# The dilated attention rebuilt for pairs of heads, and a fused bias-and-maximum pass in both attentions

## The chip, the cores and the metric

One NeuronCore of a Trainium2 chip runs the whole program. The metric is the device time of one execution in microseconds (us). The engines are TensorE (PE; PEld is its weight load), VectorE (DVE), ScalarE (ACT), GpSimd (POOL) and SyncE (SP), each with its own instruction stream; they meet only at semaphores.

## The reference

The program computes two transformer blocks over 512 tokens of width 1024 in fp32. The part that matters here is the second block, whose first layer holds a dilated attention beside a gated delta rule, and whose second layer holds a differential attention beside a gated linear attention:

```python
SWA_CONFIGS = ((128, 1), (512, 4), (2048, 16))
...
    s = jnp.einsum('bgnqhd,bgnkhd->bgnhqk', qb, kb).astype(jnp.float32) * dh ** -0.5
    s = s + bias.astype(jnp.float32)
    s = jnp.where(mask[None, None, :, None], s, -jnp.inf)
    m = jnp.max(s, axis=-1, keepdims=True)
    p = jnp.exp(s - m)
    l = jnp.sum(p, axis=-1, keepdims=True)
    o = jnp.einsum('bgnhqk,bgnkhd->bgnqhd', (p / l).astype(v.dtype), vb)
...
        s = jnp.einsum('bhcqd,bhckd->bhcqk', q_blk, kt).astype(jnp.float32) * dh ** -0.5
        s = jnp.where(dist >= 0, s + bias[None, :, None], -jnp.inf)
        p = jax.nn.softmax(s, axis=-1)
        attn = p[:, :, 0] - lam * p[:, :, 1]
```

Both attentions have 4 heads with keys of width 64. In the dilated one the three groups are merged by their log-sum-exp, which is the same as one softmax over the keys of all three. The kernel does it that way: for one head and one of the 4 residue classes of tokens (128 tokens each) there are 512 + 128 + 128 = 768 scores for each token.

## The kernel before

The program is a chain of regions, each closed by a barrier of all engines. Projections multiply in a split form (high and low parts, three matmuls, L292 to L294 and L315 to L317) with weights that SP loads ahead, ACT splits (L220) and DVE splits (L230). Around the change stand three of these regions.

`residual_region` ends with the projections for the dilated attention, "swa_qk" and "swa_v". ACT empties the banks of "swa_v" (L3193). Between the wait for the last group and its four copies ACT issues eight small DMAs (L3190), which load the bias tables of the two outer groups (`g12_bias`); four others for the inner group (`g0_bias`) are issued earlier (L3183). ACT waits at the end of the region for all twelve.

`attention` is a general softmax attention. For the dilated attention it gets 16 items, one per head and residue class. In an item PE makes three score matmuls into two PSUM banks (L620), with weights read in steps of 4 elements from `cls`; all three have the same 64 partitions for a head. DVE scales and adds the bias in three passes (L665), takes the maximum over 768 columns (L673), negates it (L676), and, when ACT has made the exponentials (L688), inverts the sums (L641) and scales all 768 columns (L651). PE turns six blocks of 128x128 (L597), ACT copies them out of PSUM in two passes (L698), PE multiplies by the values (L611, the values are the weights, the turned probabilities stream), and ACT copies the 64x128 result (L708). Scores have two pairs of banks, so PE works one item ahead: its order for step t is scores(t+1), turns(t-1), values(t-2).

`odd_mixer_region` runs the differential attention in 16 items, 4 heads times 4 query blocks with w = 128, 256, 384 and 512 keys, with the steps of the gated linear attention laid between them (on PE: inside, turn_inside, turn_keys, output, state, gla_sums). Each item has two softmaxes of width w. DVE: two bias passes (L2950, L2951), two maxima (L2954, L2956), a negation (L2958), then for the item before it the reciprocals (L2964) and two weighting passes (L2965, L2967), on which PE's turns wait (L2728). DVE's bias passes of item t wait in turn for the turns of item t-2.

The cross attention of the first block also uses `attention`, with other items.

## Time and profile before

| | before |
|---|---|
| runs | 2953.57, 2957.06, 2961.91 us (median 2957.06) |
| the profiled execution | 2957.7 us, its span 2955.4 us |
| mean granted TensorE clock | 0.958 |
| PE busy / PEld busy | 2722.0 us (92%) / 2178.0 us (74%) |
| DVE / ACT / POOL busy | 1594.1 (54%) / 1058.7 (36%) / 448.6 us (15%) |
| dilated attention, PE's first work to ACT's last copy | 1534.33 to 1614.70 us |
| attention of the odd layer, DVE's first work to its last weighting pass | 2401.28 to 2480.96 us |

PE is near full nearly everywhere, so a gain must be looked for stage by stage: in a stage in which PE is full only its own work counts, in one in which it waits the chain of waits does. A busy time of PE is modelled at its ends; starts are the surer numbers.

### The profile page before, as it was taken

What the parts mean: (1) busy time and instruction counts of PE and PEld (TensorE: products, weight loads), DVE (VectorE), ACT (ScalarE), POOL (GpSimd) and SP (SyncE); (2) the same over time, 40 slices, a digit from 0 to 9 for tenths busy, and PEclk for the clock granted to TensorE, in tenths of its full rate; (3) what the DMA queues carried; (4) which work ended last, traced back from release to release, by engine and by line L of the source; (5) the groups of instructions that cost most, each with busy time, mean ns of one, the idle gap of its engine ahead of it and who ended that gap; (6) DMA issues with size and microseconds to landing.
All of it is one profiled execution on the core that took longest, in us unless ns stands there. A gap on an engine that the chain in (4) does not pass through costs nothing. (4 is left out here: it accounts for less than half of the span.)

```text
span 2955.4 us, 33329 instructions
## 1 busy us (share of the span) xinstructions
PE 2722.0 (92%) x13110; PEld 2178.0 (74%) x13110; DVE 1594.1 (54%) x2249; ACT 1058.7 (36%) x1614; POOL 448.6 (15%) x359
## 2 busy tenths in 40 slices
PE   6998999789899999969989998899998987899997
PEld 4676999567678888746777896687786854687776
DVE  3735665444446652364435674666734256566743
ACT  4653332533342322334324343322224346422222
POOL 4544443001010000000000442000020031300002
PEclk9999899899999999989979999999999989999999
DMA  4424000433023323222220001122232210222231
GB/s 144 144 87 142 1 1 1 167 94 99 29 86 100 100 90 98 77 71 72 79 85 1 1 1 44 63 87 92 91 110 97 93 51 1 69 88 93 93 104 61
DMA packets 82626, 222.09 MB, mean 75 GB/s; under 512 B 13293, under 2 KB 29950, under 8 KB 81284
## 3 DMA queue, kind: packets, MB, share of 16 engines
q1 hardware_dynamic: 76960, 204.96, 22.0%
q10 hardware_dynamic: 5512, 15.01, 1.5%
q8 instruction: 105, 1.72, 0.2%
q14 instruction: 49, 0.39, 0.0%
HBM read 213.60 MB, written 11.58 MB: 76 GB/s over the span
## 5 line engine op out<-in xcount | busy, mean ns | idle before, releaser
L230 DVE TENSOR_TENSOR w_low<-w_raw,w_high 128x1024 fp32r<-128x1024 f32 (+2 forms) x338 | 407.2, 1206 | 884.2 <-ACT w_high L220 884.0
L292 PE MATMUL bank<-x_high,w_high 128*128 128x512 f32 x1840 | 744.9, 405 | 46.5 <-DVE x_low L486 20.4
L293 PE MATMUL bank<-x_low,w_high 128*128 128x512 f32 x1840 | 735.7, 400 | 0.0
L294 PE MATMUL bank<-x_high,w_low 128*128 128x512 f32 x1840 | 732.7, 398 | 0.0
L220 ACT ACTIVATE w_high<-w_raw 128x1024 fp32r<-128x1024 f32 (+2 forms) x380 | 386.2, 1019 | 631.6 <-PE bank L294 507.2
L292 PEld LDWEIGHTS bank<-x_high,w_high 128*128 128x128 f32 x1840 | 350.1, 190 | 159.3 <-issue 61.5
L293 PEld LDWEIGHTS bank<-x_low,w_high 128*128 128x128 f32 x1840 | 350.0, 190 | 88.1 <-issue 5.8
L294 PEld LDWEIGHTS bank<-x_high,w_low 128*128 128x128 f32 x1840 | 349.3, 190 | 83.6
L292 PE MATMUL bank<-f_high,w_high 128*128 128x512 f32 x528 | 208.8, 395 | 0.9 <-DVE w_low L230 0.9
L294 PE MATMUL bank<-f_high,w_low 128*128 128x512 f32 x528 | 209.1, 396 | 0.0
L293 PE MATMUL bank<-f_low,w_high 128*128 128x512 f32 x528 | 209.1, 396 | 0.0
L230 POOL TENSOR_TENSOR w_low<-w_raw,w_high 128x1024 fp32r<-128x1024 f32 x42 | 102.9, 2452 | 137.6 <-ACT w_high L220 137.6
L292 PEld LDWEIGHTS bank<-f_high,w_high 128*128 128x128 f32 x528 | 99.1, 188 | 27.9 <-issue 3.3
L293 PEld LDWEIGHTS bank<-f_low,w_high 128*128 128x128 f32 x528 | 99.1, 188 | 24.6 <-issue 0.5
L294 PEld LDWEIGHTS bank<-f_high,w_low 128*128 128x128 f32 x528 | 99.1, 188 | 23.2
L403 POOL TENSOR_TENSOR ln_half<-x 128x512 f32<-128x512 f32 x4 | 6.9, 1717 | 704.6 <-DVE x L3491 704.6
L3416 ACT ACTIVATE f_high<-gate 128x512 fp32r<-128x512 f32 x44 | 27.8, 632 | 215.0 <-DVE gate L3522 215.0
L292 PE MATMUL bank<-o_high,w_high 128*128 128x512 f32 x192 | 78.8, 410 | 17.6 <-DVE o_low L555 17.6
L3413 ACT ACTIVATE gate<-gate 128x512 f32<-128x512 f32 x44 | 27.8, 632 | 155.1 <-DVE gate L722 155.1
L1014 DVE TENSOR_TENSOR raw<-bank,rstd 128x512 f32<-128x512 f32 x38 | 25.9, 687 | 105.4 <-PE bank L294 80.0
L2001 POOL TENSOR_TENSOR bt<-m_ab,level_mask 128x512 f32<-128x512 f32 x48 | 65.9, 1380 | 84.5 <-PE bank L1612 83.1
L294 PE MATMUL bank<-o_high,w_low 128*128 128x512 f32 x192 | 77.4, 403 | 0.0
(593 smaller groups left out, 4319.9 us busy)
## 6 DMA issues: line engine op xcount, KB each, us to landing
w_raw<-in_ffn_in_dram SPq DMA_DIRECT2D x132, 512.0 KB, 3.4
w_raw<-in_ffn_out_dram SPq DMA_DIRECT2D x48, 512.0 KB, 3.6
w_raw<-in_gdn_in_dram SPq DMA_DIRECT2D x24, 512.0 KB, 3.4
w_raw<-in_mix_in_dram SPq DMA_DIRECT2D x22, 512.0 KB, 4.1
w_raw<-in_ffn_out_dram SPq DMA_DIRECT2D x24, 384.0 KB, 3.1
w_raw<-in_swa_qk_dram SPq DMA_DIRECT2D x12, 512.0 KB, 3.5
bias_rows<-bias_row ACTq DMA_DIRECT2D x4, 1280.0 KB, 14.0
w_raw<-in_mix_gate_a_dram SPq DMA_DIRECT2D x8, 512.0 KB, 3.4
```

What stands on the lines that cost most here:

```text
L220: self.nc.scalar.activation(self.high[c % SPLIT][:, 0:w], self.raw[c % RAW][:, 0:w], ACT.Copy).then_inc(self.high_done, 1)
L230: (on or self.nc.vector).tensor_tensor(self.low[c % SPLIT][:, 0:w], self.raw[c % RAW][:, 0:w], self.high[c % SPLIT][:, 0:w].bitcast(F32), ...
L292: nc.tensor.matmul(out, wh, high[:, k, :], start=first + at == 0, stop=False)
L293: nc.tensor.matmul(out, wh, low[:, k, :], start=False, stop=False)
L294: last = nc.tensor.matmul(out, wl, high[:, k, :], start=False, stop=first + at == depth - 1)
L403: self.nc.gpsimd.tensor_tensor(self.half[:], self.x[:, 0, :], self.x[:, 1, :], ALU.add).then_inc(self.S["half_ok"], 1)
L1014: W.freed(nc.vector.tensor_tensor(raw[i % 3][:], W.bank(PS, name, n)[:], rstd[:], ALU.mult), name, n)
L2001: nc.gpsimd.tensor_tensor(group(BT, g), group(MT[n % 2], g), mask[:, level:level + 1, :].broadcast_to([P, N, P]), ALU.mult).then_inc(R["ma ...
L3413: nc.scalar.activation(g[i % 2][:], g[i % 2][:], ACT.Silu).then_inc(R["act_ready"], 1)
L3416: nc.scalar.activation(FH[:, i, :], g[i % 2][:], ACT.Copy).then_inc(R["f_high"], 1)
```

## The change

`attention` keeps its work for the cross attention and loses the argument for loads. The dilated attention gets a region of its own, `window_region`, with 8 units, each one residue class of a pair of heads (head 0 of the pair on partitions 0 to 63, head 1 on 64 to 127):

- Scores: six matmuls, the two heads in turn, into banks 0 and 2 (the inner group) and 1 and 3 (the outer ones). There is no second set of banks: the scores of unit u+1 wait until DVE has read those of unit u.
- Logits: a fused DVE operation, `tensor_tensor_reduce`, adds the bias to the scores, multiplies by -1, and keeps the minimum, which serves as the negated maximum; ACT's exponential takes `scale=-1.0`. Two for each head: the inner 512 columns, and the outer 256, which start from the minimum of the first. The scale 1/8 moves to the queries where they are projected (`scaled_query` on DVE, and an ACT scale in the odd layer).
- Values: now the turned probabilities are the weights (128x128) and the values stream (64 columns), so the result has tokens on partitions, and DVE divides by the sums on the 128x128 result (`window_rows`) in place of scaling all columns. Four such results are turned by PE at the end of a head pair and ACT writes them out.
- Two of the three banks of turned blocks are copied by ACT, the third by DVE.
- The eight loads of `g12_bias` are issued by SP at the start of the new region, and DVE waits for the four of its head pair before the first outer pass.

The odd layer's attention takes the same fused operation for its two softmaxes (w columns each) in place of two bias passes, two maxima and a negation. The layer norms are alike in both kernels.

```diff
+def window_region(nc, C, PS, E, qk, vs, G0, G12, O, biases, masks, loaded):
...
+            for b in range(2):
+                for dst, src in biases[4 * b:4 * b + 4]:
+                    sp.dma_start(dst, src).then_inc(R[f"bias{b}"], 16)
...
+            def scores(u):
+                b, r = unit(u)
+                if u:
+                    pe.wait_ge(R["logits"], 2 * u)
+                for h in range(2):
+                    o = half(h)
+                    nc.tensor.matmul(PS[2 * h][:], cls[o, b, :, r], qk[o, 6 + b, :], start=True, stop=True)
+                for g in (1, 2):
+                    for h in range(2):
+                        o = half(h)
+                        last = nc.tensor.matmul(PS[2 * h + 1][:, chunk(g - 1)], cls[o, 2 * g + b, :, r],
+                                                cls[o, 6 + 2 * g + b, :, r], start=True, stop=True)
...
+                        last = nc.tensor.matmul(PS[7][:, o], PT[q // 4][:, chunk(q % 4)], v, start=j == 0, stop=j == PARTS - 1)
...
+            for u in range(N + 2):
+                if u < N:
+                    scores(u)
+                if u >= 2:
+                    values(u - 2)
+                if 1 <= u <= N:
+                    turn(u - 1)
+                if u >= 2 and (u - 2) % SWA_DIL == SWA_DIL - 1:
+                    finish((u - 2) // SWA_DIL)
...
+            for u in range(N + 2):
+                if 1 <= u <= N:
+                    copies(u - 1)
+                if u < N:
+                    exponentials(u)
...
+            for u in range(N + 2):
+                if u < N:
+                    logits(u)
+                if u >= 2:
+                    out(u - 2)
+                if 1 <= u <= N:
+                    last_copy(u - 1)
+                    inverse(u - 1)
...
-                steps(nc.vector.scalar_tensor_tensor(L[p][:, 0:w], PS[2 * p][:, 0:w], 64 ** -0.5, bias, ALU.mult, ALU.add))
-                nc.vector.scalar_tensor_tensor(L[p][:, w:2 * w], PS[2 * p + 1][:, 0:w], 64 ** -0.5, bias, ALU.mult,
-                                               ALU.add).then_inc(R["logits"], 1)
-                steps.wait()
-                steps(nc.vector.reduce_max(nmax[:, p, 0:1], L[p][:, 0:w], AX_X))
-                dve.wait_ge(R["logits"], t + 1)
-                steps(nc.vector.reduce_max(nmax[:, p, 1:2], L[p][:, w:2 * w], AX_X))
-                steps.wait()
-                nc.vector.tensor_scalar(nmax[:, p, :], nmax[:, p, :], -1.0, None, ALU.mult).then_inc(R["max"], 1)
+                for i in range(2):
+                    last = nc.vector.tensor_tensor_reduce(L[p][:, i * w:(i + 1) * w], PS[2 * p + i][:, 0:w], bias, -1.0, 3e38,
+                                                          ALU.add, ALU.min, nmax[:, p, i:i + 1])
+                last.then_inc(R["logits"], 1)
...
-                if gr:
-                    for dst, src in keep["biases"][1]:
-                        act.dma_start(dst, src).then_inc(R["biases"], 16)
```

PE in the middle of the dilated attention, one item and the scores that follow it, before (`logits` are the probabilities, `swa_v` the values; a matmul of this list is two records in the trace where both operands are fp32, a turn, with `ident`, is one):

```order
L620 MATMUL bank<-swa_qk_6786 128x512
L620 MATMUL bank<-swa_qk_6786 128x128 x2
L597 MATMUL bank<-ident,logits_222 128x128 x6
L611 MATMUL bank<-probs_turned_225,swa_v_6787 64x128 x6
L620 MATMUL bank<-swa_qk_6786 128x512
L620 MATMUL bank<-swa_qk_6786 128x128 x2
```

The same place after, one unit, which is the work of two items:

```order
L1465 MATMUL bank<-swa_qk_6783 128x512 x2
L1469 MATMUL bank<-swa_qk_6783 128x128 x4
L1498 MATMUL bank<-swa_v_6784,window_turned_12158 128x64 x4
L1498 MATMUL bank<-swa_v_6784,window_turned_12159 128x64 x4
L1498 MATMUL bank<-swa_v_6784,window_turned_12160 128x64 x4
L1480 MATMUL bank<-ident,window_logits_12156 128x128 x12
L1465 MATMUL bank<-swa_qk_6783 128x512 x2
L1469 MATMUL bank<-swa_qk_6783 128x128 x4
```

The score matmuls of two heads now stand beside one another, the result of a value matmul has 128 rows and 64 columns in place of 64 and 128, and the values come ahead of the turns.

ACT at the end of `residual_region` and the start of the attention, before:

```order
L220 ACTIVATE w_high_7<-w_raw_1 128x1024
L3190 DMA g_bias_6792<-bias_rows 128x128 x8
L3193 ACTIVATE swa_v_6787<-bank,rstd_cols_6795 128x4x128 x4
L543 UNCONDITIONAL_BRANCH
L681 UNCONDITIONAL_BRANCH
L688 ACT_TABLE_LOAD
L688 ACTIVATE logits_222,tot<-logits_222,nmax 128x768
```

And after:

```order
L220 ACTIVATE w_high_7<-w_raw_1 128x1024
L3346 ACTIVATE swa_v_6784<-bank,rstd_cols_6792 128x4x128 x4
L543 UNCONDITIONAL_BRANCH
L1517 UNCONDITIONAL_BRANCH
L1530 ACT_TABLE_LOAD
L1530 ACTIVATE window_logits_12156,tot_12164<-window_logits_12156,nmax_12163 128x768 x2
```

The eight DMAs have gone from between the last split of weights and the copies of `swa_v`; SP issues them behind the barrier.

DVE in the odd layer, one item with w = 384, before:

```order
L2950 SCALAR_TENSOR_TENSOR logits_19562<-bank,full_bias_6793 128x384
L2951 SCALAR_TENSOR_TENSOR logits_19562<-bank,full_bias_6793 128x384
L2954 TENSOR_REDUCE nmax_19573<-logits_19562 128x1
L2956 TENSOR_REDUCE nmax_19573<-logits_19562 128x1
L2958 TENSOR_SCALAR nmax_19573<-nmax_19573 128x2
L2984 SCALAR_TENSOR_TENSOR state_19568<-state_19568,gend_15065,bank 128x128 x2
L2964 RECIPROCAL tot_19574<-tot_19574 128x2
L2965 TENSOR_SCALAR logits_19563<-logits_19563,tot_19574,lam 128x256
L2967 SCALAR_TENSOR_TENSOR logits_19563<-logits_19563,tot_19574 128x256
```

And after, where the fused operation is printed as ISA, and each is followed by a second instruction that writes its minimum:

```order
L3112 ISA logits_19419,nmax_19430<-bank,full_bias_6790 128x384
L3112 ISA nmax_19430 128x1
L3112 ISA logits_19419,nmax_19430<-bank,full_bias_6790 128x384
L3112 ISA nmax_19430 128x1
L3140 SCALAR_TENSOR_TENSOR state_19425<-state_19425,gend_14922,bank 128x128 x2
L3120 RECIPROCAL tot_19431<-tot_19431 128x2
L3121 TENSOR_SCALAR logits_19420<-logits_19420,tot_19431,lam 128x256
L3123 SCALAR_TENSOR_TENSOR logits_19420<-logits_19420,tot_19431 128x256
```

Five instructions ahead of `state` have become four, two of them one column wide; what follows is unchanged.

## Rows read from the trace of the kernel before

**Rows 1.** Windows of both attentions: busy us (x instructions), PEclk, DMA share, GB/s.

```profile
core 0: us, PE busy (x) PEld busy (x) DVE busy (x) ACT busy (x) POOL busy (x), PEclk, DMA share, GB/s
1526.00:1534.30 8.30, 0.57 (x3) 0.26 (x2) 1.23 (x1) 3.48 (x5) 0.00 (x0) 0.70 0.49 129
1534.30:1552.00 17.70, 16.80 (x48) 11.25 (x48) 10.27 (x26) 6.11 (x11) 0.00 (x0) 0.50 0.09 28
1552.00:1562.00 10.00, 10.00 (x51) 7.73 (x51) 5.37 (x12) 4.74 (x11) 0.00 (x0) 0.94 0.00 0
2401.20:2481.00 79.80, 58.80 (x430) 37.40 (x430) 65.66 (x166) 47.77 (x142) 26.54 (x47) 0.90 0.02 5
```

**Rows 2.** Timeline, one item at full clock (start, us, engine, line; idle before).

```profile
1578.81 1.87 PEld L620 LDWEIGHTS bank<-swa_qk 64*128 64x128 f32 x6 [0.17 <-DVE logits L665]
1579.90 0.94 ACT L688 ACTIVATE logits<-logits,nmax 128x768 f32<-128x768 f32 x1 [0.59 <-DVE nmax L676]
1580.74 0.19 ACT L688 ACTIVATION_READ_ACCUMULATOR logits<-logits,nmax 128x1 f32 x1
1580.90 0.64 PEld L597 LDWEIGHTS bank<-ident,logits 128*128 128x128 f32 x6 [0.23 <-issue]
1581.71 1.28 PEld L611 LDWEIGHTS bank<-probs_turned,swa_v 128*64 128x64 f32 x12 [0.17 <-issue]
1581.88 1.09 DVE L665 SCALAR_TENSOR_TENSOR logits<-bank,g_bias 128x512 f32<-128x512 f32 x3 [1.29 <-PE bank L597]
1583.16 0.30 PEld L620 LDWEIGHTS bank<-swa_qk 64*128 64x128 f32 x1 [0.17 <-DVE logits L665]
```

**Rows 3.** Timeline, the end of the region ahead and its barrier, with the DMAs' landing.

```profile
1526.70 3.71 ACTq L3190 DMA_DIRECT2D g_bias<-bias_rows  x8
1527.76 1.23 DVE L230 TENSOR_TENSOR w_low<-w_raw,w_high 128x1024 fp32r<-128x1024 f32 x1 [4.42 <-ACT w_high L220]
1530.45 2.42 ACT L3193 ACTIVATE swa_v<-bank,rstd_cols 128x512 f32<-128x512 f32 x4 [2.73 <-issue]
1534.33 0.30 PEld L620 LDWEIGHTS bank<-swa_qk 64*128 64x128 f32 x1 [8.07 <-issue]
...
DMA to landing us min/median/max: 1.8/2.3/3.7
```

**Rows 4.** Timeline, values at half clock, and the last copy of the dilated attention.

```profile
1549.34 2.42 PEld L611 LDWEIGHTS bank<-probs_turned,swa_v 128*64 128x64 f32 x12 [0.33 <-issue]
...
1614.31 0.39 ACT L708 ACTIVATE o_even<-bank 64x128 f32<-64x128 f32 x1 [0.91 <-PE bank L611]
```

**Rows 5.** Timeline of PEld, two neighbouring loads of the outer scores.

```profile
1579.89 0.54 PEld L620 LDWEIGHTS bank<-swa_qk 64*128 64x128 f32 x2
```

**Rows 6.** Timeline of PE, score pairs of the odd layer (w = 128 and 512).

```profile
2440.02 0.30 PEld L2718 LDWEIGHTS bank<-diff_qk 64*128 64x128 f32 x4 [0.76 <-issue]
2440.02 0.49 PE L2718 MATMUL bank<-diff_qk 64*128 64x128 f32 x4
...
2454.82 1.13 PE L2718 MATMUL bank<-diff_qk 64*128 64x512 f32 x4
```

**Rows 7.** Timeline of PEld, loads of 128x128 under matmuls of 64 columns.

```profile
404.14 1.87 PEld L1534 LDWEIGHTS bank<-v_rows,m_ak 128*128 128x128 f32 x16
```

**Rows 8.** Timeline of DVE in the odd layer: items with w = 128, 384 and 512.

```profile
2462.62 0.29 DVE L2950 SCALAR_TENSOR_TENSOR logits<-bank,full_bias 128x128 f32<-128x128 f32 x1
2462.83 0.28 DVE L2951 SCALAR_TENSOR_TENSOR logits<-bank,full_bias 128x128 f32<-128x128 f32 x1
...
2463.61 0.16 DVE L2964 RECIPROCAL tot<-tot 128x2 f32<-128x2 f32 x1
...
2470.62 0.56 DVE L2950 SCALAR_TENSOR_TENSOR logits<-bank,full_bias 128x384 f32<-128x384 f32 x1 [2.21 <-PE bank L2728]
...
2474.95 0.69 DVE L2950 SCALAR_TENSOR_TENSOR logits<-bank,full_bias 128x512 f32<-128x512 f32 x1 [0.61 <-PE bank L2728]
2475.55 0.68 DVE L2951 SCALAR_TENSOR_TENSOR logits<-bank,full_bias 128x512 f32<-128x512 f32 x1
...
2477.45 0.17 DVE L2958 TENSOR_SCALAR nmax<-nmax 128x2 f32<-128x2 f32 x1
2477.53 0.16 DVE L2964 RECIPROCAL tot<-tot 128x2 f32<-128x2 f32 x1
```

**Rows 9.** Who waited for DVE's second weighting pass (L2967): us, times.

```profile
  PEld bank L2728: 23.9, 13
```

More of the change, by code:

```diff
@@ L566, in deep_blocks, with attention @@
         [(n, part)] for n in range(2, ND) for part in range(3)]
-def attention(nc, C, PS, items, width, values, loads=(), loaded=None):
+def attention(nc, C, PS, items, width, values):
     with stage(nc, "scores_ready", "logits_ready", "max_ready", "exp_ready", "probs_ready", "turned", "turned_sb",
@@ L582, in attention @@
         N = len(items)
-        @block.sync
-        def _(sp):
-            for dst, src in loads:
-                sp.dma_start(dst, src).then_inc(loaded, 16)
         @block.tensor
@@ L2703, in tile_of @@
         return t // NT, t % NT, (t % NT + 1) * P
-    with region(nc, "scores", "logits", "max", "exp", "probs", "turned", "turned_sb", "pv", "out", "own", "a_sums", "k_turned",
+    with region(nc, "scores", "logits", "exp", "probs", "turned", "turned_sb", "pv", "out", "own", "a_sums", "k_turned",
                 "o_sums", "s_sums", "d_sums", "g_sums", "rows_turned", "rows_ok", "am", "a_turned", "ker", "o", "o_sq", "d_sq", "g_read", "d_read", "log", "rstd", "at", "st",
@@ L3278, in _, with scaled_query @@
             dve.wait_ge(R["last_sq_ok"], ND)
+            def scaled_query(n):
+                W.split_low(dve, W.ahead("swa_qk", n))
+                W.wait(dve, "swa_qk", n)
+                W.freed(nc.vector.scalar_tensor_tensor(qk[:, n, :], W.bank(PS, "swa_qk", n)[:], SWA_DIM ** -0.5, rstd2[:],
+                                                       ALU.mult, ALU.mult), "swa_qk", n)
             for n in range(12):
-                scaled_to(qk[:, n, :], "swa_qk", n)
+                if n < 6:
+                    scaled_query(n)
+                else:
+                    scaled_to(qk[:, n, :], "swa_qk", n)
                 if 1 <= n < 4:
@@ L3669, in build @@
         loaded = nc.alloc_semaphore("masks_loaded")
[L3670 to L3688 removed]
+        pairs = near[1::3] + near[2::3]
+        window_region(nc, C, PS, E, qk, vs, G0, G12, OE, [pairs[i + 4 * j] for i in range(4) for j in range(2)],
+                      [(level_mask[:], A["level_mask"]), (pick[:], A["pick"])], loaded)
         recurrence_region(nc, C, PS, E, QKVZ, BETA, GAM, OE, {"level_mask": level_mask, "pick": pick, "loaded": loaded})
```

142 lines of the change are left out of this document (117 added, 25 removed).

## Prediction

> **What bounds the two stages now.** I read the windows first, then the timeline inside each stage, then who waits for whom. In the dilated attention PE is full: at half clock (PEclk 0.50) for the first 18 us, with PE 16.80 us busy of 17.70, and at full clock from about 1553 on, since the window 1552 to 1562 shows 0.94, which is 1.2 us at half [rows 1]. One item then takes 4.35 us (1578.81 to 1583.16), in which PE does scores for 2.09 us (to 1580.90), turns for 0.81 and values for 1.45 [rows 2]. PE's scores wait for DVE's bias passes by a margin that hardly shows (0.17 us), so PE's own work is the bound, and what counts is how much of it there is. The stage lasts from 1534.33 to 1614.70, 80.4 us [rows 3, 4]; 16 items of 4.35 us are 69.7, and the other 10.7 are half clock, fill and drain.
>
> In the odd layer it is otherwise. There DVE is busy 65.66 of 79.80 us, PE 58.80 and ACT 47.77 [rows 1], and PE's turns wait for DVE's second weighting pass in 13 of 16 items, 23.9 us in all [rows 9]. DVE waits back for the turns, 0.61 us in an item of 512 keys [rows 8]. The ring goes bias passes, maxima, weighting, turns, so DVE time taken out of it comes off the stage, except where another chain ends later: before the item with w = 384 DVE waits 2.21 us [rows 8], and there PE had the matmuls of the linear attention to do first.
>
> **Dilated attention, PE's work for one unit (two items).** *Scores.* Two neighbouring strided loads of the outer groups start 0.23 us apart (0.54 for two of 0.31) [rows 5], which is what an outer score record costs; the inner score streams 512 columns twice, 0.86 us for a matmul by the difference below. What two heads on different partitions do is shown in the odd layer: a pair of 128 columns takes 0.49 us and one of 512 takes 1.13, that is 0.64 for 384 columns more or 0.21 for 128, where four passes of 128 columns at 2.4 GHz are 0.21 for one matmul alone; and its four loads end after 0.30 us [rows 6]. So the pair runs side by side, loads too. I price scores at one load 0.22, the inner pair 0.86, four steps of 0.22 for the outer pairs and 0.2 of hand-over: 2.15 us, against 4.18 in two items. If the strided loads of the two halves took turns it would be eight steps, 3.0 us; with no overlap at all 4.2. I take the low value, since the pair of rows 6 has the same shape and only the step is new.
>
> *Turns.* Six load in 0.64, about 0.10 each; twelve and a hand-over are 1.4 us, against 1.62 [rows 2].
>
> *Values.* 24 records with weights of 128x128 and 64 moving columns. Sixteen such loads take 1.87 us, so 0.112 apart [rows 7]: 24 are 2.7, with the hand-over 2.85, against 2.90 now. Nothing is won there.
>
> A unit is then 6.4 us against 8.7.
>
 With the 0.11 of rows 7 for a step, a unit would be 0.55 us shorter and the stage 4.4 us; rows 5 show 0.23 for the strided one, and the sum goes by the row.
>
> *Does anything else become late?* With one set of score banks, the scores of unit u+1 wait for DVE's logits of unit u, while PE does values and turns, 4.25 us. DVE's logits are four fused passes. No trace here has the operation. Its bounds: as fast as the bias pass it replaces (0.60 from start to start at 512 columns, 0.21 at 128, so 0.34 at 256) [rows 8], or bias pass and maximum one after the other, double that. I take the first, as one pass over one PSUM and one SBUF operand. The second instruction, which writes the minimum, I put at 0.1, between the 0.08 from L2958 to L2964 [rows 8] and ACT's accumulator read of 0.19 [rows 2]. Logits: 2 x 0.60 + 2 x 0.34 + 4 x 0.1 = 2.3 us, hidden under 4.25. DVE's unit with its copy out of PSUM (as a pass of 512, 0.60), product and reciprocal is some 3.6, ACT's (two exponentials at 0.84 + 0.19 [rows 2], two copies of 512 columns taken at DVE's 0.60) some 3.3; both below 6.4. ACT begins exponentials of u only after the copies of u-1, but the turns that need them are 5 us off.
>
> *Fill, clock, drain.* Full clock came 18.9 us after PE began; I let it come after 17. At half clock values take 0.21 a load (2.42 for 12) [rows 4], 5.3 us a unit. The new order is scores 0 (3.1), a wait for the logits of 0 (2.6), scores 1, turns 0 (2.9), scores 2, and values 0 to 45% when the clock rises. That is 9.1 us of full-clock work in 17: 7.9 lost. At the end: copies out (0.9), the last product (0.35), four turns (0.6) and ACT's write (0.6), and 0.6 for the four turns in the middle: 3.1. Stage: 8 x 6.4 + 7.9 + 3.1 = 62.3 us against 80.4, so 18.1 less.
>
> *The DMAs moved.* Eight issues hold ACT from 1526.70 for 3.71 us, and its four copies start at 1530.45 in place of 1527.73, when the split is done; DVE's last split ends at 1528.99 [rows 3]. PE starts 2.7 us sooner. Its idle time then is still long enough to expect the half clock. On SP the eight come behind the barrier, ahead of both masks; nothing of the weights is queued behind them in this region. At 0.46 each the fourth is out at 1.9 us and lands 2.3 (up to 3.7) later [rows 3], at 4.2 to 5.6; DVE asks for it after 3.1 + 1.4 = 4.5. Cost 0, at most 1.1.
>
> Dilated attention and its approach: -20.8 us. The scaled queries cost nothing: one DVE pass and one ACT pass of the same size as before.
>
> **Odd layer.** From L2950 to L2964 an item takes 2.58 us at w = 512 and 0.99 at 128; two fused passes with their writes take 1.40 and 0.62 [rows 8]. Saved 1.18 and 0.37, in between on a straight line 0.91 and 0.64: 3.1 a head, 12.4 in all. I leave out the items with w = 256, whose successor is the one that waits for PE's other work: 2.6 less, so -9.8. Bounds: 5, if other chains hold half of it, and 12.4.
>
> **Sum.** 2957.7 - 20.8 - 9.8 = 2927.1 us; the execution profiled lies 0.6 above the median of the runs.
>
> **Rivals.**
> - *The strided loads of the two heads take turns.* For it: no row shows a strided pair. Against it: rows 6. Four more steps of 0.22 in 8 units, 7 us: 2934. Without any overlap of the pair 16 us: 2943.
> - *The fused pass runs at half rate.* Then a pass of 512 is 1.13, of 256 0.60: logits 3.9 us, just inside 4.25, but the fill grows by 3.2 for its two exposed logits. In the odd layer the pass costs what bias and maximum did, and 9.8 goes to about 0. Together -17.6: 2940. Its bound is the sum of the two passes of rows 8. By the Trainium skill, Vector Engine (DVE) Microarchitecture Reference, section Points that are easy to get wrong, the related accumulating form halves its rate with two fp32 operands in SBUF; here one is in PSUM, which speaks against it.
> - *Odd layer hidden.* PE, ACT and POOL chains of the linear attention end last more often, gain 2 to 4: 2934.
> - *Slower.* Each fused operation carries x us of its own. 32 lie on DVE's ring in the odd layer (32x); in a dilated unit four of them outgrow 4.25 from x = 0.49 on, 8 x (4x - 1.95), with 8x in the fill. 72x - 15.6 = 30.6 gives x = 0.64 for no change, and slower by 0.3% (8.9 us) from x = 0.76, a pass of 512 of 1.4 us with its write. For it: the kernel before never uses such an operation. Against it: all other DVE forms in rows 8 lie close to their columns.
>
> **Chances.** The forecast 0.63, loads in turn or no overlap 0.12, half rate 0.12, odd layer hidden 0.06, slower 0.05, something that eats nearly all of it 0.02. A measurement of this kernel tells about 0.3%, 9 us. All but the last two end more than 9 us below: faster 0.92, same 0.03, slower 0.05. The forecast alone reaches from 2920 (the odd layer at 12.4, clock up 4 us earlier, 2 us off the fill) to 2935 (5 in the odd layer, outer steps a little longer, bias late); with the rivals up to no overlap and half rate, 2919 to 2943.
>
> **What would show it.** In the profile after, a unit should repeat every 6.4 us with PE full (scores 2.1, values 2.85, turns 1.4); scores of 3 us mean loads in turn. A fused pass over 512 columns should last near 0.7 us, its write below 0.2. PE should start the attention 5 us after the last matmul of "swa_v", not 7.8. In the odd layer the two passes should take 1.4 us at w = 512, and DVE's waits for the turns should stay as they are or grow a little; if they grow by what the passes lose, the hidden case holds. Wrong it is if PE waits for logits in every unit, or if the clock stays at half for most of the stage.

## The result and the profile after

| | before | after |
|---|---|---|
| median of the runs | 2956.97 us (2953.57 to 2961.91, 4 runs) | 2923.73 us (2918.25 to 2927.53, 4 runs) |
| ratio | | 0.9885, 95% interval 0.9867 to 0.9903 |
| profiled execution, its span | 2957.7, 2955.4 us | 2918.25, 2916.0 us |

The changed kernel is 33.2 us faster; 30.6 was forecast (from 2957.7 to 2927.1, range 2919 to 2943). Timed again beside the last experiments it was 35.5 us faster (ratio 0.9881, interval 0.986 to 0.9902).

The two spans differ by 39.4 us. Cut at places that both traces have (starts of the first instruction of a stretch), the difference lies here:

| stretch | before | after | difference |
|---|---|---|---|
| start to ACT's first pass at L550 of the region ahead | 799.18 | 800.89 | +1.7 |
| from there to PE's first scores | 735.15 | 724.79 | -10.4 |
| dilated attention, to the next region's first load | 81.23 | 61.33 | -19.9 |
| from there to the odd layer's first scores | 785.68 | 787.57 | +1.9 |
| odd layer, to the next region's table load | 92.78 | 80.41 | -12.4 |
| the rest | 461.4 | 461.0 | -0.4 |

In the second row only 3.1 us, the shorter idle time ahead of the attention, belong to the change. The other 7.3 us go with the granted clock: in the execution of before it was lower in several windows of this stretch (0.81 from 1483 to 1503 us, 0.94 from there to 1523, 0.76 from 1293 to 1343), where the one after has 1.00, 1.00 and 0.80. Less that idle time, this stretch took 719.8 us in three profiles of the changed kernel and its variants (719.79, 719.80, 719.84) and between 725.8 and 727.8 in ten others, of both kinds of kernel. The changed kernel itself had 719.8 in one profile and 726.6 in another, so this difference is not put down to the change, though only two profiles of the old stage are at hand; single executions are to be compared by stretches.

**The dilated attention after.** Windows of the changed kernel: from PE's start to the rise of the clock, from there to the first regular unit, one unit, and the odd layer's main part:

```profile
1525.68:1534.50 8.82, 6.58 (x27) 4.12 (x28) 2.65 (x9) 3.22 (x5) 0.00 (x0) 0.50 0.50 139
1534.50:1542.39 7.89, 7.45 (x59) 6.59 (x58) 4.68 (x19) 3.68 (x8) 0.00 (x0) 1.00 0.01 2
1542.39:1548.63 6.24, 6.24 (x49) 5.61 (x49) 3.17 (x11) 2.91 (x7) 0.00 (x0) 1.00 0.00 0
2374.58:2441.80 67.22, 57.13 (x430) 36.74 (x430) 48.64 (x150) 45.46 (x142) 27.31 (x47) 0.90 0.02 6
```

They answer to [rows 1]. PE is full in a unit of 6.24 us, and half clock (0.50, the level of 1.2 GHz) has ended 8.9 us after PE's start, where the kernel before had it for 18.9. The timeline of one unit shows what fills it:

```profile
1542.39 0.55 PEld L1465 LDWEIGHTS bank<-swa_qk 64*128 64x128 f32 x4 [0.17 <-issue]
...
1543.05 1.21 PEld L1469 LDWEIGHTS bank<-swa_qk 64*128 64x128 f32 x8
...
1544.49 2.75 PEld L1498 LDWEIGHTS bank<-swa_v,window_turned 128*128 128x128 f32 x24 [0.23 <-issue]
...
1544.61 0.69 DVE L1555 CUSTOM_DVE_ANT_0 window_logits<-bank,g_bias 128x512 f32<-128x512 f32 x1 [1.35 <-PE bank L1469]
...
1545.22 0.69 DVE L1555 CUSTOM_DVE_ANT_0 window_logits<-bank,g_bias 128x512 f32<-128x512 f32 x1
...
1545.84 0.48 DVE L1562 CUSTOM_DVE_ANT_0 window_logits<-bank,g_bias,near 128x256 f32<-128x256 f32 x1
...
1546.24 0.48 DVE L1562 CUSTOM_DVE_ANT_0 window_logits<-bank,g_bias,near 128x256 f32<-128x256 f32 x1
...
1547.11 1.35 PEld L1480 LDWEIGHTS bank<-ident,window_logits 128*128 128x128 f32 x12
...
1548.63 0.55 PEld L1465 LDWEIGHTS bank<-swa_qk 64*128 64x128 f32 x4 [0.17 <-issue]
```

Scores last 2.10 us (1542.39 to 1544.49), values 2.62, turns 1.52; two items took 8.70 [rows 2]. DVE's four fused passes are done at 1546.7, two microseconds before PE's next scores: those stand behind an idle time of 0.17 us in which they wait for no other engine. At the start of the stage the same passes are seen with the instructions that write the minimum:

```profile
1529.36 0.08 DVE L1555 DVE_READ_ACCUMULATOR2_ANT near<- 128x1 f32 x1
1529.36 0.69 DVE L1555 CUSTOM_DVE_ANT_0 window_logits<-bank,g_bias 128x512 f32<-128x512 f32 x1
```

A write of 0.08 us starts in the same moment as the pass behind it and adds nothing to the time between two passes. A pass over 512 columns starts 0.61 us before the next, as a plain bias pass did [rows 8].

The end of the stage, PE's loads (with one line of its matmuls, which names what the values wait for) and then ACT:

```profile
1575.58 2.75 PEld L1498 LDWEIGHTS bank<-swa_v,window_turned 128*128 128x128 f32 x24 [1.08 <-issue]
1575.61 2.86 PE L1498 MATMUL bank<-swa_v,window_turned 128*128 128x64 f32 x24 [0.88 <-DVE window_turned L1578]
...
1580.63 2.75 PEld L1498 LDWEIGHTS bank<-swa_v,window_turned 128*128 128x128 f32 x24 [1.08 <-issue]
1583.98 0.42 PEld L1504 LDWEIGHTS bank<-ident,window_rows 128*128 128x128 f32 x4 [0.59 <-DVE window_rows L1572]
1587.01 1.13 PEld L2246 LDWEIGHTS bank<-gam,pick 6*128 6x128 f32 x5 [2.62 <-issue]
```

```profile
1584.67 1.07 ACT L1541 ACTIVATE o_even<-bank 128x512 f32<-128x512 f32 x1 [4.64 <-PE bank L1504]
```

PE waits 1.08 us for DVE's copy of the third bank twice, 0.59 for the last product, and 2.62 at the barrier behind ACT's write of 1.07 us.

**The approach.** ACT and PE at the end of the region ahead, which answer to [rows 3]:

```profile
1522.06 2.40 ACT L3346 ACTIVATE swa_v<-bank,rstd_cols 128x512 f32<-128x512 f32 x4
...
1525.68 0.58 PEld L1465 LDWEIGHTS bank<-swa_qk 64*128 64x128 f32 x4 [5.00 <-issue]
```

PE's loads idle 5.00 us in place of 8.07; ACT's copies begin with the end of its last split (1522.1).

**The odd layer.** DVE in the first head, items with w = 384 and 512, and who waited for the second weighting pass; they answer to [rows 8, 9]:

```profile
2388.01 0.56 DVE L3112 CUSTOM_DVE_ANT_0 logits<-bank,full_bias 128x384 f32<-128x384 f32 x1 [4.60 <-PE bank L2889]
...
2391.67 0.69 DVE L3112 CUSTOM_DVE_ANT_0 logits<-bank,full_bias 128x512 f32<-128x512 f32 x1 [0.64 <-PE bank L2889]
...
2392.29 0.69 DVE L3112 CUSTOM_DVE_ANT_0 logits<-bank,full_bias 128x512 f32<-128x512 f32 x1
...
2392.90 0.16 DVE L3120 RECIPROCAL tot<-tot 128x2 f32<-128x2 f32 x1
```

```profile
  PEld bank L2889: 9.9, 12
```

PE's waits for the weighting fell from 23.9 us in 13 items to 9.9 in 12. The times from the first pass of one head to that of the next:

| head | before | after | gained |
|---|---|---|---|
| 1 | 21.60 | 19.53 | 2.1 |
| 2 | 20.05 | 15.32 | 4.7 |
| 3 | 18.86 | 15.31 | 3.6 |
| 4, to the region's end | 31.40 | 29.39 | 2.0 |

### The profile page after: what moved, and what is told of

It reads as the page before. It is cut to its first block and busy times, and to the rows that moved or that the text cites. A ratio compares the mean times of both kernels' runs of the same rounds, so it can differ in the third digit from the quotient of the medians.

```text
span 2916.0 us, 33247 instructions
## 1 busy us (share of the span) xinstructions
PE 2693.7 (92%) x13118; PEld 2163.4 (74%) x13118; DVE 1557.8 (53%) x2209; ACT 1045.6 (36%) x1584; POOL 449.5 (15%) x359
## 5 line engine op out<-in xcount | busy, mean ns | idle before, releaser
L292 PE MATMUL bank<-x_high,w_high 128*128 128x512 f32 x1840 | 743.2, 404 | 46.5 <-DVE x_low L486 20.4
L292 PE MATMUL bank<-o_high,w_high 128*128 128x512 f32 x192 | 78.1, 407 | 17.3 <-DVE o_low L555 17.3
L293 PE MATMUL bank<-o_low,w_high 128*128 128x512 f32 x192 | 77.6, 404 | 0.0
```

Source lines behind the costliest of these rows:

```text
L292: nc.tensor.matmul(out, wh, high[:, k, :], start=first + at == 0, stop=False)
L293: nc.tensor.matmul(out, wh, low[:, k, :], start=False, stop=False)
```

## The experiments

The theory: the dilated attention gains because PE runs two heads side by side, the approach because eight issues no longer hold ACT, and the odd layer because DVE's time is taken off the ring. Rivals: the fused pass or the shorter instruction list makes the gain; the parts help each other; the barrier waited for something else. Twelve kernels ran in three sets of four, the first on one chip and the other two on another, each beside the kernel before. Four were timed more than once (the two parts alone and the last two timed against one another); the other eight have one execution each, so of them the stages are compared and not the total.

**One part alone.** First the kernel before with only the odd layer's fused pass:

```diff
-                steps(nc.vector.scalar_tensor_tensor(L[p][:, 0:w], PS[2 * p][:, 0:w], 64 ** -0.5, bias, ALU.mult, ALU.add))
...
-                nc.vector.tensor_scalar(nmax[:, p, :], nmax[:, p, :], -1.0, None, ALU.mult).then_inc(R["max"], 1)
+                for i in range(2):
+                    last = nc.vector.tensor_tensor_reduce(L[p][:, i * w:(i + 1) * w], PS[2 * p + i][:, 0:w], bias, -1.0, 3e38,
+                                                          ALU.add, ALU.min, nmax[:, p, i:i + 1])
+                last.then_inc(R["logits"], 1)
```

> The kernel before, with the fused pass in the odd layer's attention alone. Theory (DVE time taken off the ring comes off the stage): the odd layer's region, from DVE's first work to the region's end, 91.6 us before and 79.2 us with the whole change, should take 79 to 80 here too, the dilated attention stays at 81 us, and the kernel lies 12 us below the kernel before, ratio 0.996. Rival (part of the odd layer's gain belongs to something else in the change, a different clock or a different start): 3 to 6 us less than before, and DVE's waits for the turns grow by what the passes lose.

Measured: ratio 0.997, interval 0.9955 to 0.9985 (median 2950.80 against 2955.59, 7 and 10 runs). Between the marks of the table above the odd layer took 80.45 us (before 92.78, with the whole change 80.41), so the theory's 12 us are there in the profiled execution. It was the fastest of the seven (2940.72 to 2951.95 us), and the ratio of the medians is worth 8.9 us, with 12 inside its interval. The dilated attention took 78.66 us in place of 81.23 although nothing in it was changed: its clock rose 16.7 us after PE's start, not 18.9. That is how far two executions of the old stage differ.

Then the whole change with this part of the diff undone:

> The whole change with the odd layer's fused pass undone. Theory: the dilated attention takes 61 us and the idle time of PE's loads ahead of it 5.0 us, as in the whole change, the odd layer takes 91.6 us as before, and the kernel lies 12.4 us above the changed kernel and 20 to 23 below the kernel before, ratio 0.992 to 0.993. Together with the run of the fused pass alone the two parts should add up to the whole (33 us). Rival (the parts help each other, since a lighter odd layer also keeps the clock up): the two parts add up to clearly less than 33 us.

Measured: ratio 0.9931, interval 0.991 to 0.9951 (2938.25 us, 4 runs). The dilated attention took 61.34 us, the idle time ahead of it 5.00, the odd layer 94.04. By the ratios the two parts are worth 8.9 and 20.4 us of 2955.6, together 29.3, against 34.0 (0.0115) for the whole: their intervals (4.4 to 13.3 and 14.5 to 26.6) hold the difference. By the stretches they are 12.3 for the one, 3.1 and 17.3 to 19.9 for the other, together 33 to 35, less 1.4 us by which the region behind the attention is longer (787.03 against 785.68). The odd layer is 1.3 us longer than in the kernel before at granted clocks of 0.85, 0.98 and 0.91 in its last three stretches of 20 us, where that had 0.91, 1.00 and 1.00; with the fused pass it is 1.00 in both stretches of 20 us behind the first (three executions). By the stretches the parts help each other by no more than that; the intervals of the ratios alone would not exclude more.

**Is it the fusion?** Unfused passes in the new stage:

```diff
-                    nc.vector.tensor_tensor_reduce(L[p][:, h, 0:S], PS[2 * h][:], G0[:, hd, 3 - r:3 - r + S], -1.0, 3e38,
-                                                   ALU.add, ALU.min, near[:, p, h:h + 1]).then_inc(R["near"], 1)
+                    nc.vector.tensor_tensor(L[p][:, h, 0:S], PS[2 * h][:], G0[:, hd, 3 - r:3 - r + S],
+                                            ALU.add).then_inc(R["near"], 1)
...
+                for h in range(2):
+                    dve.wait_ge(R["near"], 6 * u + 3 + h)
+                    nc.vector.reduce_max(near[:, p, h:h + 1], L[p][:, h, :], AX_X).then_inc(R["near"], 1)
+                dve.wait_ge(R["near"], 6 * u + 6)
+                nc.vector.tensor_scalar(nmax[:, p, :], near[:, p, :], -1.0, None, ALU.mult).then_inc(R["logits"], 2)
```

> The whole change, but the dilated attention adds its bias in four plain passes, takes a maximum over 768 columns for each head and negates, in place of the fused passes; the same results. DVE's logits of a unit then last about 4.0 us (2 x 0.60 + 2 x 0.34 + two maxima over 768 columns of about 0.85 + 0.1 to 0.3) in place of 2.3. Theory (PE's own work is what the new stage saves, the fusion is no more than cover): a unit stays at 6.2 to 6.5 us, the fill grows by about 3 us for the two exposed logits, and the stage takes 64 to 66 us in place of 61.3. Rival (the fused pass makes the gain): a unit grows by what the logits grow, 1.7 us, and the stage takes 73 to 75 us.

PE's loads in the steady part of that kernel:

```profile
1550.86 0.55 PEld L1465 LDWEIGHTS bank<-swa_qk 64*128 64x128 f32 x4 [0.17 <-DVE nmax L1567]
...
1552.96 2.75 PEld L1498 LDWEIGHTS bank<-swa_v,window_turned 128*128 128x128 f32 x24 [0.23 <-issue]
```

The next scores start at 1557.09: a unit of 6.23 us, and the stage took 65.99. The wait is still 0.17 us, but its releaser is now DVE's negation: logits of 3.9 us (1553.08 to 1557.02) just fit under values and turns (4.14). So the fusion is worth 4.7 us of this stage, all in the fill (PE waited 4.05 and 1.30 us for the first two logits, against 2.21 and 0.44, which is 2.7 us, and the clock rose 13.0 us after the start, not 8.9, which is some 2 more), and nothing in the units.

**Is it the side-by-side running?** Two edits of the score loop. With the heads in turn:

```diff
-                for g in (1, 2):
-                    for h in range(2):
-                        o = half(h)
+                    for g in (1, 2):
                         last = nc.tensor.matmul(PS[2 * h + 1][:, chunk(g - 1)], cls[o, 2 * g + b, :, r],
                                                 cls[o, 6 + 2 * g + b, :, r], start=True, stop=True)
```

And with both heads on one half of the partitions, at both places that have it:

```diff
-                    o = half(h)
+                    o = half(0)
```

> The whole change, with the score matmuls of a unit in another order: all three of head 0, then all three of head 1, so that only one place in a unit has matmuls on different partitions beside one another. Theory (the gain comes from two heads running side by side on PE): the scores of a unit take 3.5 to 4.2 us in place of 2.1, the unit 7.7 to 8.3 in place of 6.24, and the stage 73 to 78 us in place of 61.3, so that nearly all of the stage's gain of 19.9 us is gone. Rival (the gain comes from fewer instructions and hand-overs, from the order of the stage and from DVE): the scores take 2.1 to 2.5 and the stage 61 to 64 us.

Measured: a unit of 7.32 us (1551.91 to 1559.23), scores 3.18, stage 71.73. All three numbers missed: some 60% of the overlap is gone, not all (3.18 against 2.10 with it and 3.89 without, below). The loads show why:

```profile
1551.91 0.54 PEld L1465 LDWEIGHTS bank<-swa_qk 64*128 64x128 f32 x2 [0.17 <-issue]
1552.57 0.74 PEld L1467 LDWEIGHTS bank<-swa_qk 64*128 64x128 f32 x2
1553.00 0.30 PEld L1465 LDWEIGHTS bank<-swa_qk 64*128 64x128 f32 x1
1553.21 0.33 PEld L1467 LDWEIGHTS bank<-swa_qk 64*128 64x128 f32 x1
1553.21 0.33 PEld L1465 LDWEIGHTS bank<-swa_qk 64*128 64x128 f32 x1
1553.44 1.42 PEld L1467 LDWEIGHTS bank<-swa_qk 64*128 64x128 f32 x5
1555.09 2.75 PEld L1496 LDWEIGHTS bank<-swa_v,window_turned 128*128 128x128 f32 x24 [0.23 <-issue]
```

Head 1's inner loads (L1465, at 1553.00 and 1553.21) lie among head 0's outer ones (L1467): the last matmul of one head still runs beside the first of the other. So the second edit was made:

> The whole change, but the score matmuls of head 1 read the partitions of head 0 (0 to 63), so head 1 of each pair gets the scores of head 0 and the output differs; number, shape and order of all instructions stay. Theory (two heads on different partitions run side by side, and that is what the new stage gains): the scores of a unit take 4.2 us as in two items of the kernel before, a unit about 8.3 us, and the stage 76 to 79 us, against 61.3 with the change and 78.7 to 81.2 in the two profiled executions that have the old stage: at least three quarters of the stage's gain are gone. Rival (order, instruction count and hand-overs bring a good part): a unit of 7.3 us or less, as with the heads in turn, and a stage below 73.

Windows of that kernel, and a unit's score loads at full clock:

```profile
1546.00:1550.00 4.00, 4.00 (x14) 2.96 (x13) 0.76 (x2) 2.07 (x5) 0.00 (x0) 0.87 0.01 4
1550.00:1570.00 20.00, 20.00 (x80) 17.15 (x80) 5.59 (x20) 3.02 (x6) 0.00 (x0) 0.51 0.00 0
1574.00:1580.00 6.00, 6.00 (x43) 5.58 (x43) 2.86 (x10) 1.32 (x3) 0.00 (x0) 1.00 0.01 3
1530.22:1628.18 97.96, 91.14 (x392) 76.21 (x392) 25.39 (x88) 27.40 (x51) 0.01 (x1) 0.67 0.05 13
```

```profile
1579.45 1.39 PEld L1465 LDWEIGHTS bank<-swa_qk 64*128 64x128 f32 x4 [0.17 <-issue]
1580.97 2.13 PEld L1469 LDWEIGHTS bank<-swa_qk 64*128 64x128 f32 x8
1583.34 0.30 PEld L1498 LDWEIGHTS bank<-swa_v,window_turned 128*128 128x128 f32 x2 [0.23 <-issue]
```

At full clock scores take 3.89 us and a unit 8.03 (1571.42 to 1579.45), near what the theory has (4.2 and 8.3) and far from the rival. The stage took 97.96 us, 17 more than the old one, which neither expected: the clock rose 16.9 us after the start, fell back at 1550.5, and was at half for most of the stage (mean 0.67). Eight units of 8.03 in place of 6.24 explain 14.3 of the 36.6 us lost; the other 22 are what is left over, and go with the clock. So at full clock the side-by-side running makes 1.79 of the 2.46 us by which a unit is shorter than two old items, some three quarters. The other 0.67 (scores 4.18 to 3.89, values 2.90 to 2.62, turns 1.62 to 1.52) belong to the new order and to values with the probabilities as weights; no run takes these apart. As the stage ran, clock included, nothing of its gain was left.

**What sets the pace of the outer scores?** The loads in steps of four elements, or the streams in such steps? The next edits answer that; in the first two other tokens or keys are scored.

Dense weights:

```diff
-                    nc.tensor.matmul(PS[2 * h][:], cls[o, b, :, r], qk[o, 6 + b, :], start=True, stop=True)
+                    nc.tensor.matmul(PS[2 * h][:], qk[o, b, chunk(r)], qk[o, 6 + b, :], start=True, stop=True)
...
-                        last = nc.tensor.matmul(PS[2 * h + 1][:, chunk(g - 1)], cls[o, 2 * g + b, :, r],
+                        last = nc.tensor.matmul(PS[2 * h + 1][:, chunk(g - 1)], qk[o, 2 * g + b, chunk(r)],
```

Dense streams:

```diff
-                                                cls[o, 6 + 2 * g + b, :, r], start=True, stop=True)
+                                                qk[o, 6 + 2 * g + b, chunk(r)], start=True, stop=True)
```

> The whole change, but the weights of all score matmuls are read from 128 neighbouring columns in place of every fourth one, so other tokens are scored and the output differs; the moving operands stay as they are (the outer ones in steps of four). Theory (a strided load costs 0.22 us a step and sets the scores): the four outer pairs take four steps of 0.11 to 0.17, the scores 1.5 to 1.8 us in place of 2.1, a unit 5.7 to 5.9 us in place of 6.24. Rival, for which the Trainium skill speaks (page TensorE: Matmul & The Clock Gate, section LDWEIGHTS: the load time follows the number of columns), by rows: the step in the loads does not matter and the strided streams set the pace, so scores stay at 2.1 and the unit at 6.2.

> The whole change, but the moving operands of the outer score matmuls are read from 128 neighbouring columns, so other keys are scored and the output differs; the weights stay in steps of four. Theory (the strided loads set the scores): nothing changes, scores 2.1 and unit 6.24 us. Rival (the strided streams set them): scores 1.7 and unit 5.8 us. If both this and dense weights alone leave 2.1, both must be dense to win, since a load and a stream of 0.22 run beside one another.

The first execution of the dense streams ran at a granted clock of 0.647 from end to end (3863.91 us) and tells nothing; it was repeated:

> The changed kernel with the moving operands of the outer score matmuls read from 128 neighbouring columns once more (other keys are scored, the output differs), since the execution before it ran at a mean granted clock of 0.647. From the runs since: with dense weights alone the scores went from 2.1 to about 1.96 us and the unit to 6.10, with both dense to 1.50 and 5.64. Theory (load and stream of an outer matmul run beside one another, and the longer of the two sets the pace): with dense streams alone the strided loads of 0.22 set it, so scores 1.95 to 2.1 and a unit of 6.1 to 6.24 us. Rival (the stream's step alone costs, the load's does not): scores 1.5 to 1.6 and a unit of 5.65 to 5.75.

And both together, in a kernel in which DVE sorts queries and outer keys by class when it writes them:

```diff
+            by_class = qk[:].rearrange("p k (r i) -> p k i r", r=SWA_DIL)
+
+            def tokens(t):
+                return t[:].rearrange("p (i r) -> p i r", r=SWA_DIL)
...
-                W.freed(nc.vector.scalar_tensor_tensor(qk[:, n, :], W.bank(PS, "swa_qk", n)[:], SWA_DIM ** -0.5, rstd2[:],
-                                                       ALU.mult, ALU.mult), "swa_qk", n)
+                W.freed(nc.vector.scalar_tensor_tensor(by_class[:, n], tokens(W.bank(PS, "swa_qk", n)), SWA_DIM ** -0.5,
+                                                       tokens(rstd2), ALU.mult, ALU.mult), "swa_qk", n)
```

> The whole change, and DVE writes the projected queries and the keys of the outer groups sorted by residue class, so that PE reads every score operand from neighbouring columns; the same result. DVE's writes then go in steps of 128 elements, and its reads of the bank in steps of four. Theory (the step of four in PE's operands is what the outer scores cost): scores 2.1 to 1.5 us (inner pair 0.86, four steps of 0.11 to 0.13, hand-over), a unit 6.24 to 5.6 to 5.75 us, the stage 61.3 to 56.5 to 58 us, and DVE's passes of the projection (0.6 us each) do not get longer. Rival (DVE's strided writes cost what PE saves): the passes grow to 1 us or more, and the approach to the attention gets 1 to 4 us longer. Rival (another step sets the unit, as DVE's logits or the values): a unit of 6.0 us or more.

The outer pairs' loads and matmuls (eight records each) and the start of the values, first with dense weights, then dense streams, then both:

```profile
1553.55 1.07 PE L1469 MATMUL bank<-swa_qk 64*128 64x128 f32 x8
1553.55 0.65 PEld L1469 LDWEIGHTS bank<-swa_qk 64*128 64x128 f32 x6 [0.24 <-issue]
...
1554.55 0.19 PEld L1498 LDWEIGHTS bank<-swa_v,window_turned 128*128 128x128 f32 x1 [0.35 <-issue]
```

```profile
1548.22 1.21 PEld L1469 LDWEIGHTS bank<-swa_qk 64*128 64x128 f32 x8
...
1548.64 0.97 PE L1469 MATMUL bank<-swa_qk 64*128 64x128 f32 x8
...
1549.55 0.19 PEld L1498 LDWEIGHTS bank<-swa_v,window_turned 128*128 128x128 f32 x1
```

```profile
1541.62 0.61 PE L1469 MATMUL bank<-swa_qk 64*128 64x128 f32 x8
1541.62 0.42 PEld L1469 LDWEIGHTS bank<-swa_qk 64*128 64x128 f32 x6 [0.23 <-issue]
...
1542.16 0.19 PEld L1498 LDWEIGHTS bank<-swa_v,window_turned 128*128 128x128 f32 x1
```

| | scores | of these ahead of the outer matmuls | outer matmuls | unit | stage |
|---|---|---|---|---|---|
| after | 2.10 | 1.09 | 1.01 | 6.24 | 61.33 |
| dense weights | 1.96 | 0.96 | 1.00 | 6.10 | 64.21 |
| dense streams | 1.99 | 1.08 | 0.91 | 6.13 | 60.74 |
| both, sorted by DVE | 1.50 | 0.96 | 0.54 | 5.64 | 58.21 |

Either edit alone gains 0.11 to 0.14 us a unit, both together 0.60. What dense weights alone gain lies ahead of the outer matmuls, which keep their pace. A pair here is one record of each head, and a unit has four such pairs: the load of one pair runs beside the stream of another, and while one of the two has steps of four it sets 0.23 to 0.25 us a pair (the column of the outer matmuls by four); dense, a pair takes 0.14. My theory for the first edit (1.5 to 1.8) and the rival of the third (1.5 to 1.6) are both out; the expectation that the longer of the two sets the pace held. The stage with dense weights alone is longer in spite of its shorter unit since its clock was at half once more, from about 1576 to 1582 us (0.50 in the window from 1576.09 to 1581.09), behind a wait of 1.13 us for the write of the first head pair. The sorted kernel shortens the stage by 3.1 us, to 0.2 above the range that was expected. DVE's ten projection passes grew from 0.68 to 1.08 us, as the rival had it and not the theory, but the stretch ahead did not grow (719.84 us): they hide under PE's projections.

**Timed against the changed kernel.**

> The changed kernel itself, for comparison with the sorted version on one chip: ratio to the kernel before 0.9885 within 0.002. In its profile the region ahead of the attention, from ACT's first pass over the outputs to the last projection, takes either 719.8 or 726 to 727 us, as in the executions so far, and the dilated attention 61.3 us.

> The changed kernel with queries and outer keys sorted by residue class by DVE, timed in five rounds. By its profile its dilated attention takes 58.2 us in place of 61.3: 3.1 us below the changed kernel, that is 0.001 lower in ratio, 0.9874 to 0.9876 of the kernel before where the changed kernel has 0.9885. Rival (what PE gains is lost in other executions through a later clock or longer DVE passes): no difference between the two.

Measured: the changed kernel 2922.94 us, ratio 0.9881 (0.986 to 0.9902); sorted 2919.31, 0.9878 (0.9854 to 0.9903). The stages again differ by 3.1 us (61.34 and 58.23), and both profiles have the longer stretch ahead (726.6 and 725.9); the timing can't tell the two kernels apart, since four runs of one kernel spread over 7 to 8 us.

**The approach.** The eight loads go back to ACT, ahead of its copies of "swa_v":

```diff
-            for b in range(2):
-                for dst, src in biases[4 * b:4 * b + 4]:
-                    sp.dma_start(dst, src).then_inc(R[f"bias{b}"], 16)
...
+                if gr:
+                    for dst, src in keep["late_biases"]:
+                        act.dma_start(dst, src).then_inc(R["biases"], 16)
```

> The whole change, but the eight bias loads go back to ACT, between its wait for the last bank of the value projection and its copies, and ACT waits for them at the region's end as before. Theory (the eight issues hold ACT's copies and so PE): the idle time of PE's loads ahead of the dilated attention goes from 5.0 back to 7.7 to 8.1 us, and SP's eight issues of 3.65 us vanish from the stage, which stays at 61.3 us or, where the clock comes up later, up to 1 us more. Rival (the barrier waited for something else as well): idle time of 5.0 to 6.5 us.

```profile
1518.89 3.71 ACTq L3341 DMA_DIRECT2D g_bias<-bias_rows  x8
...
1522.65 2.42 ACT L3344 ACTIVATE swa_v<-bank,rstd_cols 128x512 f32<-128x512 f32 x4 [2.73 <-issue]
...
1526.73 0.57 PEld L1462 LDWEIGHTS bank<-swa_qk 64*128 64x128 f32 x4 [8.28 <-issue]
```

Idle time 8.28 us in place of 5.00 (a little above the 7.7 to 8.1 expected, and far from the rival's 5.0 to 6.5), stage 60.93. The stretch ahead less this idle time is 719.80 us, with the loads on SP 719.79: the eight issues cost 3.3 us and nothing else in the approach moves.

## Why the prediction was right, step by step

The sum had -18.1 for the dilated attention, -2.7 for its approach and -9.8 for the odd layer; the stretches show -19.9, -3.1 and -12.4, and +1.9 that it did not have. The side-by-side running, the freed ACT and the shorter ring were each found where they were forecast. That the total came within 3 us is in part luck: a fill that was priced 3.0 us too high and a drain 2.1 too low, an odd layer 2.6 too low and a loss behind the attention of 1.9 stand against one another.

- **PE's own work is the bound and side-by-side pairs cut it.** Right, by the one-half experiment, which gives the pairs some three quarters of what a unit gained. Scores 2.10 (forecast 2.15), turns 1.52 (1.4), values 2.62 (2.85), a unit 6.24 (6.4): 1.3 us over eight units. The loads did get shorter when dense (two inner pairs 0.30 in place of 0.55 us), so the measurement decides against that rule; but dense weights alone saved only 0.14 us a unit, since the strided streams, which I had not priced, hold the pace by themselves (outer matmuls 1.00 us in place of 1.01). The Trainium skill's page SBUF — State Buffer, section Specifications (TRN2), gives a reason that fits both: lines of 16 bytes, with a penalty for each crossing, which a step of four fp32 elements makes at every element. No run here varies the step, so that stays an argument.
- **Clock and fill, 7.9 us lost.** Mis-sized: 4.9, by what is left of 60.1 us (PE's start to the end of ACT's last write) after 49.9 for the units and 5.2 for waits at the end. I let the clock rise 17 us after the start, near the 18.9 of before; it rose after 8.9, and after 8.3 to 9.6 in the seven other profiles with the same order (without the unfused passes). No row of before said so.
- **Drain 3.1 us.** Mis-sized the other way: 5.2 (0.9 beyond the usual hand-over twice, 1.1 in the middle: four turns, and values that wait 0.87 us, for the write of the first head pair; 2.4 behind the last values). ACT's write of the 128x512 result takes 1.07 us, not 0.6 as its dense copies of that size; it writes in steps of four, which may be the reason but was not tried. With fill and drain together the stage came out 2.2 us shorter than forecast (60.1 against 62.3).
- **The fused pass runs at its columns' rate, its write costs 0.1.** Right on the rate (0.61 from start to start at 512 columns; at 256 it is 0.34 in the odd layer, as forecast, and 0.40 in the dilated attention; 0.21 at 128); the write costs nothing. The rival at half rate is out. That the pass hides in the units was shown by the unfused kernel, whose 3.9 us of logits hide too.
- **The DMAs moved, -2.7, bias wait 0.** 3.1 in the two profiles, 3.3 by the experiment. DVE never waited for the tables.
- **Odd layer, -9.8.** Measured 12.4, where the sum's own upper bound was, by two errors of opposite sign that leave 2.6. DVE's time for a head fell by 4.1 us, not 3.1 (busy 17.30 to 13.20 in the second head). The writes are free, 0.2 us an item. And at w = 256 the five old instructions took 2.06 to 2.09 us in the first three heads, where the straight line has 1.52, and 1.52 in the fourth; what differs is the negation of two columns, in the second head and in the fourth:

```profile
2431.45 0.71 DVE L2958 TENSOR_SCALAR nmax<-nmax 128x2 f32<-128x2 f32 x1
...
2467.40 0.17 DVE L2958 TENSOR_SCALAR nmax<-nmax 128x2 f32<-128x2 f32 x1
```

  GpSimd is busy 7.7 us and more in each of the first three heads and not at all in the fourth; that this is the cause was not tried. Against the larger saving stands what I left out: I took one wait, 2.21 us in the last head, for all four. In heads 2 and 3 the old wait at w = 384 was 0.49, so there nearly the whole saving came through (of the 4.7 us of head 2 some belong to the clock, 0.92 before and 1.00 after; head 3 had 1.00 in both and gained 3.6). In heads 1 and 4 it is partly hidden, as the waits for the turns at w = 384 grew from 1.86 to 4.60 and from 2.21 to 3.19 us.
- **What the sum did not have: +1.9 us behind the attention.** The next region's first 16 us ran at half clock:

```profile
1587.01:1603.01 16.00, 13.24 (x56) 12.17 (x57) 8.51 (x20) 3.10 (x10) 5.20 (x5) 0.50 0.00 1
```

```profile
1611.90:1627.90 16.00, 12.03 (x61) 10.66 (x61) 8.97 (x21) 4.32 (x15) 6.05 (x6) 0.68 0.00 1
```

The second row is the same stretch behind the old stage, in the kernel with only the odd layer's fused pass, at 0.68. Behind the new stage the clock fell at 1585.8 us, in the middle of the 2.62 us in which PE idles at the barrier; PE idles 1.53 there before, and the clock fell 2.6 us after the next region had begun. From this mark to the odd layer ten profiles with the new stage took 787.0 to 788.1 us (with both heads on one half 786.3), the two with the old stage 784.9 and 785.7: the loss recurs, and the prediction had no term for it. That the longer idle time is its cause was not tried.

## What to carry to other kernels

Where two matmuls have 64 rows each, put their operands on different halves of the partitions and issue them in turn: the pair costs about what one costs (scores 2.10 us against 3.89). Then look at the steps of both operands, since one strided operand is enough to hold the pace, and let the engine that writes them sort them if it has cover (3.1 us of the stage here, too little to be seen in the time of the whole kernel). Price the end of a stage with the same care as its middle, and look at the clock of the stage behind it as well.

## What was not expected of the hardware

- The same stage drew different clocks, even where its instructions were the same. In the dilated attention the granted clock rose 18.9 and 16.7 us after PE's start with the old order, 8.3 to 9.6 with the new one, 13.0 with unfused passes, 15.6 with the heads in turn, and with both heads on one half it rose after 16.9 us and fell again at 1550.5, when PE had been busy 4.00 of the last 4.00 us shown (1546 to 1550). Which property of the work decides it is open.
- The second instruction of the fused operation (0.08 us) starts together with the next pass and delays nothing.
- A DVE pass over two columns, the old negation, took 0.71 to 0.74 us at w = 256 in three heads and 0.17 in the fourth.
- DVE passes of 512 columns that read a PSUM bank and write SBUF in another order took 1.08 in place of 0.68 us.
- One execution ran at a granted clock of 0.647 throughout, with the same program that at the next attempt had 0.958.
